# GpSimd's w_lo subtraction issued as four instructions of 256 columns instead of one of 1024

## Time and profile before

| | us |
|---|---|
| median of 3 runs | 3807.3 (3805.75 to 3810.4) |
| the profiled execution, its own time | 3809.84 |
| its span in the trace | 3808.1 |
| PE busy | 3536.4 (93%) |
| DVE busy | 1755.7 (46%) |
| ACT busy | 1211.6 (32%) |
| POOL busy | 1295.1 (34%), of it w_lo 1199.5 in 476 instructions |
| mean granted clock of the PE | 0.938 |

### The profile page before, as it was taken

How to read it: one execution, slowest core, us unless ns; L and a number is a source line. 1 busy time by engine, 2 the same in 40 slices (tenths; PEclk the granted TensorE clock), 3 DMA queues, 4 the chain that set the end, 5 groups by cost and what they waited for, 6 DMA issues and landing times.

```text
span 3808.1 us, 48842 instructions
## 1 busy us (share of the span) xinstructions
PE 3536.4 (93%) x17570; PEld 2897.4 (76%) x17570; DVE 1755.7 (46%) x2490; ACT 1211.6 (32%) x1974; POOL 1295.1 (34%) x544
## 2 busy tenths in 40 slices
PE   8999999999999999997989879999999979689998
PEld 6668877777668887776767768788887867677887
DVE  5434368886534358887145453311212144543223
ACT  3333332223333332223334432312222334333222
POOL 3214434443214444442221242223332221333443
PEclk9999999999999999997999968999999989779999
DMA  3112244442112234443211222111111211322222
GB/s 137 59 39 99 94 144 154 154 153 93 61 38 89 98 129 154 154 154 112 89 61 34 73 79 78 47 64 61 63 63 55 100 61 40 109 100 78 95 94 99
DMA packets 94036, 348.32 MB, mean 91 GB/s; under 512 B 10256, under 2 KB 10512, under 8 KB 92112
## 3 DMA queue, kind: packets, MB, share of 16 engines
q1 hardware_dynamic: 70416, 256.51, 20.2%
q10 hardware_dynamic: 23488, 90.02, 6.9%
HBM read 337.91 MB, written 8.59 MB: 91 GB/s over the span
## 4 chain that ended last, share of the span: by engine, by line
issue 54%; POOL 19%; PE 18%; DVE 5%; ACT 2%; DMA 1%; POOLq 0%; ACTq 0%; DVEq 0%; SPq 0%
POOL w_lo L468 19%; PE ps L822 3%; PE ps L823 3%; PE ps L824 3%; PE ps L1033 1%; PE ps L914 1%; PE ps L915 1%; PE ps L916 1%; PE ps L897 1%; DVE tiny L2096 1%; ACT sn L1425 1%; DMA m_row<-m_spill 1%; ACT pn L1392 1%; PE ps L1024 0%; DVE m_row L2129 0%
## 5 line engine op out<-in xcount | busy, mean ns | idle before, releaser
L468 POOL TENSOR_TENSOR w_lo<-w_raw,w_hi 128x1024 fp32r<-128x1024 f32 x476 | 1199.5, 2521 | 2341.6 <-ACT w_hi L1137 2325.9
L1137 ACT ACTIVATE w_hi<-w_raw 128x1024 fp32r<-128x1024 f32 x472 | 499.3, 1058 | 859.0 <-PE ps L824 446.1
L822 PE MATMUL ps<-c_hi,w_hi 128*128 128x512 f32 x1248 | 450.3, 361 | 32.3 <-DVE c_lo L1966 24.3
L823 PE MATMUL ps<-c_lo,w_hi 128*128 128x512 f32 x1248 | 446.4, 358 | 0.0
L824 PE MATMUL ps<-c_hi,w_lo 128*128 128x512 f32 x1248 | 442.9, 355 | 0.0
L543 PE MATMUL ps<-h_hi,w_hi 128*128 128x512 f32 x976 | 388.8, 398 | 0.0
L544 PE MATMUL ps<-h_lo,w_hi 128*128 128x512 f32 x976 | 383.3, 393 | 0.0
L545 PE MATMUL ps<-h_hi,w_lo 128*128 128x512 f32 x976 | 382.8, 392 | 0.0
L822 PEld LDWEIGHTS ps<-c_hi,w_hi 128*128 128x128 f32 x1248 | 239.9, 192 | 84.0 <-DVE c_lo L1966 21.4
L1884 DVE SCALAR_TENSOR_TENSOR ada_junk<-ada_w,c_silu 128x1024 f32<-128x1024 f32 x192 | 297.6, 1550 | 3.3
L823 PE MATMUL ps<-u_lo,w_hi 128*128 128x512 f32 (+1 forms) x768 | 273.5, 356 | 0.0
(11 more groups left out here) (330 smaller groups left out, 6138.3 us busy)
## 6 DMA issues: line engine op xcount, KB each, us to landing
w_raw<-in_w SPq DMA_DIRECT2D x476, 512.0 KB, 3.3
ada_w<-in_ada ACTq DMA_DIRECT2D x96, 512.0 KB, 4.5
m_row<-m_spill ACTq DMA_DIRECT2D x16, 768.0 KB, 6.7
wq_row<-wq_spill ACTq DMA_DIRECT2D x16, 384.0 KB, 5.6
x_spill<-x ACTq DMA_DIRECT2D x2, 2048.0 KB, 6.3
bias<-in_rpb ACTq DMA_DIRECT2D x8, 512.0 KB, 3.3
x<-x_spill ACTq DMA_DIRECT2D x2, 2048.0 KB, 7.9
c<-in_c SPq DMA_DIRECT2D x1, 2368.0 KB, 13.6
```

Source lines behind the costliest of these rows:

```text
L468: nc.gpsimd.tensor_tensor(w_lo[:, j, :], w_raw[:, j % RAW, :], w_hi[:, j, :].bitcast(F), ALU.subtract).then_inc(lo_ready, 1)
L822: nc.tensor.matmul(bank, w_hi[:, j, w], hi[:, part], start=(k == ends[0]), stop=False)
L823: nc.tensor.matmul(bank, w_hi[:, j, w], lo[:, part], start=False, stop=False)
L1137: nc.scalar.activation(w_hi[:, j, :], w_raw[:, j % RAW, :], ACT.Copy).then_inc(hi_ready, 1)
```

## The change

`lower` issues the subtraction of one chunk as four instructions of 256 columns each. The last of the four counts up `lo_ready`; the wait ahead of the first stays as it is. The constant `LOWER` is new. Nothing else is changed.

```diff
 RING, RAW = 4, 2
+LOWER = 256
...
                 pool.wait_ge(hi_ready, g * RING + (j + 1))
-                nc.gpsimd.tensor_tensor(w_lo[:, j, :], w_raw[:, j % RAW, :], w_hi[:, j, :].bitcast(F),
-                                        ALU.subtract).then_inc(lo_ready, 1)
+                for a in range(0, KT * P, LOWER):
+                    c = slice(a, a + LOWER)
+                    last = nc.gpsimd.tensor_tensor(w_lo[:, j, c], w_raw[:, j % RAW, c], w_hi[:, j, c].bitcast(F), ALU.subtract)
+                last.then_inc(lo_ready, 1)
```

## The result

The changed kernel takes 3746.15 us (median of 4 runs, 3744.03 to 3749.57) against 3807.67 us for the kernel before in the same comparison: a ratio of 0.9839, 95% interval 0.9822 to 0.9856, 61.5 us less. Forecast were 3749 us in a range of 3724 to 3790. The profiled execution's span is 3747.8 us (before 3808.1), its mean granted clock 0.943 (before 0.938). In the code after the change every line behind `lower` stands 3 further down: the square is L1907, `u_lo` L1900, the dot products L1887, the matmuls of the down half L788 to L790, and the subtraction L471.

A forecast was written before the change was run, and what follows sets the result against it. PE, busy 93%, was taken to be limited by its waits for DVE's u_lo, held up by POOL, and by the clock falling after them. -30 - 20 - 10 + 2 = -58 us from the median gave 3749 us, range 3724 to 3790.

The forecast's parts named there:

- The change from up to down: Block 1's MLP, eight changes: PE's waits for u_lo shrink from 5.45 to 1.6 us each, -30 us (-18 to -41).
- The clock: PE's clock around those eight changes stays up in most, recovering two thirds of 31 us: -20 us, bounds 0 and -31.
- The first rival: At the changes the stalls shrink but the clock does not come back: -38 us, 3769 us, chance 0.20.
- Elsewhere: Mod copy at layer ends, first softmaxes, squares ahead of block 2's norms: DVE held less, -10 us, bounds -3 and -13.
- costs: Slower w_lo shows at the start, at two empty chunks and partly in the mLSTM: +2 us, bound +4.
- POOL's price: POOL's subtraction: 0.70 us per 256 columns, a chunk 2.8 us instead of 2.33, 220 us more POOL time over 476 chunks.
- The second rival: POOL's next piece goes before the waiting DVE instruction, so nothing is gained: 3813 us, chance 0.08.
- The third rival: Up halves: late w_lo delays the w_raw load, ACT's split and u_hi behind it: slower, 3840 us, chance 0.06.
- The 12 us of cover: Slot refill in the other 470 chunks: w_lo is hidden while PE works on three other chunks, some 12 us spare.

The follow-up runs named there:

- e1: The kernel before, with four pieces only in block 1's MLP groups and one instruction of 1024 columns everywhere else: 3758.76 us, ratio 0.9863.
- e2: The kernel before, with four pieces everywhere except in block 1's MLP groups, which keep one instruction of 1024 columns: 3800.98 us, ratio 0.9978.
- e8: The changed kernel (256 columns), with ACT making u_hi ahead of the next weight chunk's split in block 1's up halves: 3744.21 us, ratio 0.983.
- e4: The changed kernel with eight pieces of 128 columns in place of four of 256: 3841.1 us, ratio 1.0086 to the kernel before.
- e5: The changed kernel, but POOL subtracts only columns 0 to 255 of each chunk, the other 768 columns' lower part being zero: 3682.21 us, ratio 0.9663.
- e11: The changed kernel, with ACT issuing the three ada_w loads behind the relu of j = 3 in block 1's up halves: 3745.01 us, ratio 0.9821.

## Why the prediction was right, step by step

**The change from up to down, -30 us.** Measured: 45.2 to 13.8 us of waits, 31.4 us. The steps hold, and that the total came so close is in part luck: the copy came less early than forecast and the eighth `u_lo` earlier, and the two cancel. The copy came 2.3 us earlier (forecast 2.7, bounds 1.6 and 3.7), and so did the relu and the seventh `u_lo`, at fixed distances as forecast: PE waits 1.35 us in place of the forecast 0.9. The eighth `u_lo` came 3.9 us earlier (10.60 to 6.68 us behind PE's start of the half), and PE waits 0.16 us, forecast 0.7. The two first changes of a layer, which the prediction took to be like the rest, wait longer, 2.00 and 2.40 us.

**The clock, -20 us.** Two thirds of 31 us was a choice between two bounds and not worked out; that it fits is luck. e1 gives 18 us as what is left of 50.4 us behind 32.2 of waits, and PE's busy time fell by 16.6 us there and by 14.5 in the whole change. By the prediction's own arithmetic, (1 - clock) x 14 over the eight windows, it would be 31 before and (3 x 0.12) x 14 = 5 after, 26 us. That arithmetic also books half speed where PE only waits, so it overstates both. The first rival, the clock that does not come back, is refuted by the five windows at 1.00.

**Elsewhere -10, costs +2.** e2 gives -8.2 us. The sum is right, its parts are not all: of the softmaxes, whose first waits were forecast to shrink, those of block 1 (L686) grew from 3.9 to 5.9 us, while those of block 2 (L900, for ACT's `pn`) fell from 11.1 to 4.2, the largest fall of one line; the waits before norms (L587 9.6 to 6.0, and L811 on DVE's squares 5.5 to 1.3) shrank by 7.8. The waits for `w_lo` itself cost 2.2 us, forecast 1.4 for the three places.

**POOL's price.** A free piece costs 0.70 us, as forecast. But w_lo grew by 449 us (1199.5 to 1648.2), not by 220: each of four pieces can meet a DVE instruction, where one did before. The prediction had that (5 us per chunk in the up halves) and rightly cost it at nothing. In e1's MLP groups the mean is 1127 ns, 4.5 us per chunk:

```profile
L471 POOL TENSOR_TENSOR w_lo<-w_raw,w_hi 128x256 fp32r<-128x256 f32 x512 | 560.5, 1127 | 186.0 <-ACT w_hi L1144 186.0
```

The wait of ACT for `w_raw` was put at about 1.5 us per chunk, with a load that lands in 3.3 us. It is 2.6 us in the mean and 6.4 at most, in part because loads meet the `ada_w` loads, which no step of the prediction has. It costs nothing that can be seen (e8); the load shown above lands at 653.7, when the last `u_hi` of the half is long made.

**The second rival, the pieces hold as one:** refuted by DVE's squares (926 ns; the longest is 1.27 us) and by the two dot products inside POOL's run of six. Getting in between has a price for DVE too, which the prediction did not name: the dot products, held now and then before (mean 1550 ns against 1.21 us free), now meet a piece more often, if a shorter one, and rose to 1602 ns.

**The third rival, DVE starves POOL:** wrong at 256 columns, right at 128. Its threshold was given as a w_lo of over 7.3 us, from the margin of a single load. In e4 a chunk of the up half takes 5.7 us in the mean, just over PE's 5.45 us, and the kernel loses all the same: POOL's lag grows over the up half, by its pieces and by the late load in the middle, and ACT's split passes it on to `u_hi`. The 12 us of cover that the prediction named lie between `w_lo` and PE. They do nothing for `u_hi`, which stands behind the split.

**Where my theories missed** was in the experiments around it. For e4 the longer chunk was named (6.5 us and more), but a loss of at most 19 us on the changed kernel was expected from it, and 95 came. For e5 a gain of 4 to 11 us was expected from the remaining holds, and 64 us came, most of it not from the waits in question. For e11 the relu was let run free, but the issues still waited for DVE's copy, which was late.

## What to carry to other kernels

A DVE instruction with both inputs in SBUF waited for whatever was left of the running POOL instruction. Cutting POOL's instruction made that wait shorter, moving one DVE operand to PSUM took it away for that instruction, and together they gained most. Of the four sizes tried 256 columns is best (1024, 512, 256, 128: 3808, 3786, 3746, 3841 us), since every cut adds a fixed cost and one more place where DVE holds POOL. So before cutting, compare POOL's contended time per chunk with the time in which the consumer uses a chunk, look at what stands behind POOL's last piece in the other engines' orders, and at which other loads are under way when the next load is issued.

## What the runs showed that I had not expected

- The holds are mutual and symmetric in effect: six pieces that would take 4.2 us alone took 7.08 us beside two dot products, and these took 1.75 and 1.64 us in place of 1.21.
- The smaller POOL's pieces, the more their fixed part and DVE's holds weigh together: eight pieces of 128 columns average 557 ns each (1980.2 us in all), four of 256 898 ns (1648.2), two of 512 1473 ns (1382.9), one of 1024 2521 ns (1199.5). Without a DVE instruction beside them eight pieces of 128 take 3.40 us (e4 at 593.36) and four of 256 2.82.
- Small DVE instructions are held too. The `mod` copy of 6 columns took 0.47 us in the timeline above where 0.17 is its free price, and 2.10 us once in the kernel before.
- A `w_raw` load beside three `ada_w` loads took 7.3 us to land, alone 3.3. A change of POOL's instructions, which leaves every transfer as it was, brought them together.
